# A hybrid decoder step on one core: the router's weights loaded through GpSimd's queue, and the last expert block's down product in four input slices

## The reference, cut to what matters

```python
mk, mv = _mem_kv(mem_prompt, norm_mem_g, w_ck, w_cv, ck_norm_g)       # memory keys and values
z = _rms(x, norm_g) @ w_in                                            # 2048 x 3584
...
lg = (h @ w_rg) + b_rg            # w_rg: 2048 x 4,  router over 4 groups
le = (h @ w_re) + b_re            # w_re: 2048 x 32, router over 32 experts
...
def expert_block(args):           # 2048 -> 512 -> 2048
    xe, e = args
    a = jax.nn.silu(xe @ w_e_gate[e]); b = xe @ w_e_up[e]
    return (a * b) @ w_e_down[e]
y = zeros.at[buf_t].add(yb * buf_g[:, None])
```

## Time and profile before

| | us |
|---|---|
| median of 3 runs | 1541.58 |
| lowest, highest run | 1539.56, 1543.03 |
| the profiled execution's own time | 1531.4 |
| its span in the trace | 1529.6 |
| PE busy | 1269.7 (83%) |
| DVE busy | 531.1 (35%) |
| ACT busy | 167.7 (11%) |
| POOL busy | 62.6 (4%) |

### The profile page before, as it was taken

The page is one execution under the profiler, slowest core; times in us unless marked ns, Lnnn a source line. Parts: engine busy times, 40 slices in busy tenths (PEclk is TensorE's granted clock), DMA queues, the critical chain, the costliest instruction groups (busy, mean ns, idle before and its releaser), DMA issues.

```text
span 1529.6 us, 23145 instructions
## 1 busy us (share of the span) xinstructions
PE 1269.7 (83%) x9913; PEld 626.5 (41%) x9913; DVE 531.1 (35%) x1102; ACT 167.7 (11%) x395; POOL 62.6 (4%) x115
## 2 busy tenths in 40 slices
PE   7799999998999999887867777777787677778777
PEld 4354458774887866322222222222222222222222
DVE  1040064750112334534334333433433433333344
ACT  0410012321111244000000000000000000000000
POOL 2000012212010000000000000000000000000000
PEclk9899999999999999988888788878887878778789
DMA  9999999989999999999999999999999999999997
GB/s 346 316 332 399 327 329 382 382 311 375 379 399 400 359 389 355 403 429 426 429 433 426 430 432 431 425 429 434 425 429 434 425 429 434 425 429 429 431 428 309
DMA packets 101909, 609.34 MB, mean 398 GB/s; under 512 B 11390, under 2 KB 13065, under 8 KB 78929
## 3 DMA queue, kind: packets, MB, share of 16 engines
q1 hardware_dynamic: 55027, 477.14, 75.0%
q10 hardware_dynamic: 38822, 101.11, 18.1%
q0 software_dynamic: 8016, 30.46, 5.7%
HBM read 603.09 MB, written 106.75 MB: 464 GB/s over the span
## 4 chain that ended last, share of the span: by engine, by line
DMA 53%; PE 40%; ACTq 3%; DVE 1%; issue 1%; ACT 1%; SPq 1%; DVEq 0%
DMA ring<-in_w_e_up_dram 44%; PE pb L1157 12%; PE pb L663 6%; PE pb L909 6%; DMA ring<-in_w_out_dram 5%; DMA ring<-in_w_in_dram 4%; PE pb L745 4%; ACTq L1286 2%; PE pb L1041 2%; PE pb L927 2%; PE pb L713 1%; SPq L486 1%; PE pb L669 1%; PE pb L1016 1%; PE pb L1191 1%
## 5 line engine op out<-in xcount | busy, mean ns | idle before, releaser
L1157 PE MATMUL pb<-ring,xT 128*32 128x256 f32 x4096 | 285.7, 441 | 123.4 <-DMA ring<-in_w_e_up_dram 118.7
L1157 PEld LDWEIGHTS pb<-ring,xT 128*32 128x32 f32 x4096 | 143.5, 126 | 285.7 <-DMA ring<-in_w_e_up_dram 156.5
L2040 DVE TENSOR_TENSOR Z<-pb,Z 128x512 f32<-128x512 f32 x248 | 152.7, 679 | 253.1 <-PE pb L1110 253.1
L1093 PE MATMUL pb<-Z,xT 128*32 128x512 f32 (+1 forms) x768 | 137.1, 808 | 94.8 <-DVE Z L2040 91.7
L1110 PE MATMUL pb<-xT 32*128 32x512 f32 x744 | 168.7, 751 | 0.0
L1191 PE MATMUL pb<-ring,xT 128*32 128x512 f32 x960 | 136.9, 722 | 0.0
L663 PE MATMUL pb<-ring,hreg 128*128 128x512 f32 (+1 forms) x320 | 125.7, 552 | 2.6 <-DMA ring<-in_w_in_dram 2.6
L1093 PEld LDWEIGHTS pb<-Z,xT 128*32 128x32 f32 (+1 forms) x768 | 16.6, 117 | 185.7 <-DVE Z L2040 118.9
L663 PEld LDWEIGHTS pb<-ring,hreg 128*128 128x128 f32 x320 | 60.1, 190 | 65.1 <-issue 59.2
L909 PE MATMUL pb<-hreg,ring 128*128 128x264 f32 x320 | 78.3, 402 | 5.8 <-DMA ring<-in_w_out_dram 5.8
L745 PE MATMUL pb<-hreg,ring 128*128 128x264 f32 x320 | 75.3, 395 | 1.0 <-DMA ring<-in_w_in_dram 1.0
(11 more groups left out here) (333 smaller groups left out, 1117.2 us busy)
## 6 DMA issues: line engine op xcount, KB each, us to landing
ring<-in_w_e_gate_dram SPq DMA_DIRECT2D x61, 2048.0 KB, 18.6
ring<-in_w_e_up_dram SPq DMA_DIRECT2D x61, 2048.0 KB, 23.1
ring<-in_w_e_down_dram SPq DMA_DIRECT2D x30, 4096.0 KB, 18.9
out_win_k_sample_dram<-in_cache_win_k_dram ACTq DMA_DIRECT2D x24, 1536.0 KB, 15.4
out_win_v_sample_dram<-in_cache_win_v_dram ACTq DMA_DIRECT2D x24, 1536.0 KB, 14.0
ring<-in_w_in_dram SPq DMA_DIRECT2D x7, 4096.0 KB, 32.9
ring<-in_w_out_dram SPq DMA_DIRECT2D x4, 4096.0 KB, 32.7
out_win_k_sample_dram<-in_cache_win_k_dram ACTq DMA_DIRECT2D x8, 1488.0 KB, 15.0
```

Of the source, the lines that this page charges most:

```text
L1093: last = mm(pb[0][32 * c:32 * c + 32, :], pick[0:n, t, :], xn[0:n, t, 512 * c:512 * c + 512], start=(t == 0), stop=(t == 2))
L1157: last = mm(pb[1][32 * c:32 * c + 32, 0:256], XT[:, k, :], w[:, :, k8, P * c:P * c + P], start=(k == 0), stop=(k == KT - 1))
L2040: last = V.tensor_tensor(d, banks[c][:, :], d, ALU.add)
```

## The change

Three things change. The loads of w_rg, w_re and b_re go from ACT's queue to POOL's, behind the bias loads. The last block's down weights are loaded in four input slices over all 2048 columns, and PE multiplies all four column groups for a slice, then ACT copies the whole output at once and `results()` goes through the tiles one after the other; DVE's adds and SP's stores follow that order (both halves of tile 0, then tile 1). And PE multiplies the identity with itself 14 times ahead of the last block's gate and up products.

```diff
 SP
-            for q in range(4):
-                c, f = slice(1024 * (q // 2), 1024 * (q // 2) + 1024), slice(2 * (q % 2), 2 * (q % 2) + 2)
-                sp.dma_start(slot2.rearrange("p (k n) -> p k n", k=4)[:, f, c], w[:, f, c]).then_inc(last_landed[q], 16)
+            for f in range(4):
+                sp.dma_start(slot2[:, D * f:D * f + D], w[:, f]).then_inc(last_landed[f], 16)
...
-            for n, t, hf in ((1, 0, 0), (2, 1, 0), (3, 0, 1), (5, 1, 1)):
+            for n, t, hf in ((1, 0, 0), (2, 0, 1), (3, 1, 0), (5, 1, 1)):
 POOL
+            for w, lo, n in (("w_rg", 0, NG), ("w_re", NG, NE)):
+                pool.dma_start(wr[:, :, lo:lo + n], a[w][0].rearrange("(k p) n -> p k n", p=P)).then_inc(router_landed, 16)
+            pool.dma_start(b36[:, NG:36], a["b_re"].to_broadcast([P, NE])).then_inc(router_landed, 16)
             pool.wait_ge(pads_ready, 1)
 PE
-            def results(hf):
+            def results():
-                for t in ((0, 1), (0, 2, 1))[hf]:
+                for t in range(3):
                     if t == 2:
                         pe.wait_ge(x_final, 1)
-                    for c in range(4) if t == 2 else (2 * hf, 2 * hf + 1):
+                    for c in range(4):
                         ...
-                    last.then_inc(out_filled, 1)
+                        if c == 3 or c == 1 and t < 2:
+                            last.then_inc(out_filled, 1)
...
+                if last_of_all:
+                    for _ in range(14):
+                        mm(pb[1][:, 0:P], ident[:], ident[:], start=True, stop=True)
...
-                pe.wait_ge(last_landed[0], LAST_LANDED[0])
-                last_down(0, (0, 1), pb[3])
-                pe.wait_ge(last_landed[1], LAST_LANDED[1])
-                last_down(0, (2, 3), pb[3]).then_inc(dn_used, 1)
+                for f in range(4):
+                    pe.wait_ge(last_landed[f], LAST_LANDED[f])
+                    for c in range(4):
+                        last = mm(pb[3][32 * c:32 * c + 32, :], aT[:, 32 * f:32 * f + 32],
+                                  slot2[:, D * f + 512 * c:D * f + 512 * c + 512], start=(f == 0), stop=(f == 3))
+                last.then_inc(dn_used, 1)
                 pe.wait_ge(gt_ready, NE)
-                pe.wait_ge(last_landed[2], LAST_LANDED[2])
-                last_down(1, (0, 1), pb[2])
                 pe.wait_ge(y_added, 3 * (NE - 1))
                 pe.wait_ge(yo_ready, NE)
-                results(0)
-                pe.wait_ge(last_landed[3], LAST_LANDED[3])
-                last_down(1, (2, 3), pb[2]).then_inc(dn_used, 1)
-                pe.wait_ge(yo_ready, NE + 1)
-                results(1)
+                results()
 ACT
-            for w, lo, n in (("w_rg", 0, NG), ("w_re", NG, NE)):
-                act.dma_start(wr[:, :, lo:lo + n], a[w][0].rearrange("(k p) n -> p k n", p=P)).then_inc(router_landed, 16)
-            act.dma_start(b36[:, NG:36], a["b_re"].to_broadcast([P, NE])).then_inc(router_landed, 16)
             act.wait_ge(zeros_ready, 2)
...
-                act.wait_ge(dn_used, NE)
-                nc.scalar.copy(yo[0:64, :], pb[3][0:64, :]).then_inc(yo_ready, 1)
-                act.wait_ge(dn_used, NE + 1)
-                nc.scalar.copy(yo[64:P, :], pb[2][64:P, :]).then_inc(yo_ready, 1)
+                block_out(NE - 1)
 DVE
-                for n, (hf, t) in enumerate(((0, 0), (0, 1), (1, 0), (1, 2), (1, 1))):
-                    dve.wait_ge(out_filled, n + 1)
+                for n, hf, t in ((1, 0, 0), (2, 1, 0), (3, 0, 1), (5, 0, 2), (4, 1, 1)):
+                    dve.wait_ge(out_filled, n)
```

## The result

The changed kernel takes 1523.25 us (median of 4 runs, 1516.14 to 1531.43), the kernel before 1541.47 beside it (1539.56 to 1543.03): a ratio of 0.9893, 95% interval 0.9861 to 0.9926. That is 18.2 us less, where 9.7 were forecast. The profiled execution took 1516.14 us, 15.3 less than that of before.

What follows compares the result with a forecast made beforehand. Bound: TensorE work for 610 us, then expert weight loads; the change touches only the ends, the start held by ScalarE's 30.33 us issue. Start -10.7 plus end +1.0 gives -9.7: 1541.58 to 1531.9 us, range 1527.5 to 1538.5.

Steps and rivals of the forecast that it cites:

- What bounds the start: First 40 us: ScalarE's 30.33 us issue of L1286 delays squares and diagonals, leaving TensorE idle 9.86 us before L705.
- 3.64 us at half speed held 1.82 us of work at full speed, a gain of 1.82 us: Start, 53.02 to 56.7: without TensorE's stop the slow-clock stretch goes too, saving 1.82 us besides the idle 9.86.
- its deduction: Start: 1 us taken off the 11.7 us gain for short rows on the DMA engines, leaving -10.7 us.
- I take 1: Start: router loads' short rows beside cache copies and perhaps the second w_in piece cost 1 us, bounds 0 and 5.
- I take nothing: Start: earlier cache copies might delay the memory values' weights, losing up to 5 us; 0 was taken.
- The end: Last block: identity products cost 3.2 us, down product to last add gains 2.2; sum +1.0 us, bounds -0.7 and +2.5.
- I carry this over: Whole kernel: the runs' median stays 10.2 us above the profiled execution, giving 1531.9 us instead of 1521.7.
- 1.5 us for the spread of the runs: Whole kernel: allowance of 1.5 us for run spread in the range 1527.5 to 1538.5, given 0.82.
- the best of every bound: Forecast case's lower limit, -12.4 us, with both the start's and the end's bounds at their best.
- the shift was to travel through it: Between start and end: events release the work, so a shift of the start reaches the end if loads keep up.

Runs made afterwards that it cites:

- The front alone: Kernel before with only the three router loads moved from ScalarE's queue to POOL's: 1522.17 us, ratio 0.9913; a second time 1524.83 us, ratio 0.9912.
- the end alone: Changed kernel with the three router loads put back on ScalarE's queue, so only the last block differs from the kernel before: 1538.78 us, ratio 1.0021.
- the kernel with identity products in the wait: Kernel before with 42 identity products added between TensorE's bias products and its wait for the diagonals: 1533.99 us, ratio 0.9970.
- the first pair: First profiles of the changed kernel and the kernel before; the changed kernel's median was 1523.25 us against 1541.47, ratio 0.9893.
- the three comparisons: The same changed kernel measured three times beside the kernel before: 1523.25 us (ratio 0.9893), 1525.39 us (0.9933) and 1521.55 us (0.9905).

## Why the prediction was wrong in size and right in mechanism

*What bounds the start: right.* With the long issue gone, the squares, the diagonals and the scales follow as forecast; the idle 9.86 us are gone, with 9 us of cover at the diagonals instead of 1.5 to 5.4. The front alone carries the gain, the end alone loses, and with the lists on SP's queue ScalarE is free and the scales start at 43.34 all the same: what held the start up was ScalarE's issue.

*The step that failed: "3.64 us at half speed held 1.82 us of work at full speed, a gain of 1.82 us".* The mechanism is right (the kernel with identity products in the wait shows it by itself), the size was that of one execution. In four traces with the blocked start the slow stretch cost 1.7 to 5.0 us, 3.1 in the mean, and the wait before it ended 0.6 to 0.9 us later in the three others. The first w_in product comes at 93.2 to 97.2 with the start blocked (mean of four 95.3) and at 81.3 to 82.8 with it free (mean of eight 81.9): the start is worth 13.3 us, where the forecast had 11.7 before its deduction. Of the difference 1.3 us are the slow stretch, most of the rest the later end of the wait. Of the terms of the sum this one was off most, and still it makes only 1.6 of the 8.5 us by which the forecast fell short.

*"I take 1" for the short rows: too much.* TensorE's wait for the second w_in piece did not grow (0.81 us before, 0.18 after). A price of 3 to 6 us may be there at the first piece, where it is hidden. Its source was misread in part: with the short rows gone from the first 40 us, the window from 15 to 20 still moves only 291 GB/s in the changed kernel (269 before); that from 35 to 40 moves 378 (248 before).

*"The values' weights: I take nothing": right, but the wrong load was watched.* They land at 38.7 instead of 39.4. The copies, issued 19 us earlier, hit the next load instead, the first w_in piece (13.2 to 37.8 us), which the forecast took as a proof that copies do little. That piece was down to its last 3 us when the first copies came. It cost nothing by luck of 2 us of cover.

*The end: right.* Forecast +1.0; 26.88 against 26.15 in the first pair is +0.73, and over the six traces with the changed end (26.81 to 27.06) against the three of before and the first with the front alone (26.14 to 26.15) it is +0.8; the second with the front alone has 25.77. (The kernel that keeps the clock up is left out: there TensorE's restart waits for weights.) The identity instructions took 4.82 us (forecast 4.9), the first half behind them 3.66, the down product 3.64, each as forecast.

*"I carry this over": the 10.2 us between the profiled execution and the median.* That execution, 1531.4 us, was quicker than each of the 55 timed ones of before (the lowest 1531.52; medians from 1536.48 to 1541.47). The two later profiles of before took 1539.66 and 1536.83. A part of the 6 us by which it was quick is its short slow stretch: the failed step again. The difference to the kernel before, which is what was missed, does not hang on it.

*"1.5 us for the spread of the runs": too little.* The four runs of the changed kernel spread over 15.3 us, the interval of the ratio alone reaches from 11.4 to 21.4 us, and the three comparisons lie 7.1 us apart. The range's lower edge, 1527.5, was the best of every bound with this 1.5 us; in it the start could not turn out better than read from the first trace, and it did.

*What stays open.* The three comparisons gave -18.2, -11.1 and -16.7, in the mean -15.3. The terms as measured give -13.3 + 0.8 = -12.5. Between start and end lies a long stretch for which the forecast had no term of its own: the shift was to travel through it. The traces have, in us (mean and range):

| from, to | start blocked, 4 traces | start free, 8 traces |
|---|---|---|
| first w_in product, cross-attention product near 512 to 534 | 437.0 (435.5 to 438.9) | 434.3 (430.7 to 437.7) |
| that product, TensorE's restart | 972.5 (971.3 to 974.8) | 973.9 (971.3 to 976.7) |

So 2.7 us are won in the first part and 1.3 lost again in the second; at the restart the free traces are 14.7 us ahead. In both parts the ranges overlap, and an earlier start need not be the reason: two kernels that are in neither mean, with the clock kept up (first w_in product at 92.74) and with the lists on SP's queue (89.15), took 433.9 and 433.2 us for the first part, like the free ones.

Of the 8.5 us that the forecast missed, 2.8 are its own terms (start 1.6, short rows 1.0, end 0.2), 1.4 this stretch, 1.4 what the mean of the comparisons has beyond the traces, and 2.9 what the first comparison has beyond that mean. For the last three no cause is shown.

## What to carry to other kernels

Lists of some thousand short rows are paid by the engine that hands them out, here 30 us and more on two hardware queues and 2.9 on POOL's: look for one long issue bar, ask who needs that engine in the meantime, and move the list to the engine that nobody waits for; moved to another busy queue it only changes the victim. Before a term is taken from one trace, ask whether it depends on when something happened to start: a clock's slow stretch and waits for loads do, and want two or three traces. When a queue is unblocked, list everything that it will now send earlier, and look for the load that used to run alone.

## What the runs showed of the hardware

The same three loads made far more packets on the hardware queue than on POOL's. The DMA queues over the whole run (packets, MB, share), first before, then after:

```profile
q10 hardware_dynamic: 38822, 101.11, 18.1%
q0 software_dynamic: 8016, 30.46, 5.7%
```

```profile
q10 hardware_dynamic: 34550, 100.80, 17.9%
q0 software_dynamic: 8176, 30.78, 5.9%
```

4272 packets left ScalarE's queue and 160 came to POOL's, for the same 0.3 MB. On SP's queue (q1) the lists made 4272 packets too: 58787 in that run, 54515 in the changed kernel. With them went the long issue (30.33 us on ScalarE, 36.95 on SP, 1.16 on POOL) and the late landing (35.4, 47.8 and 14.6 us). The Trainium skill, page "DMA: Bandwidth & Descriptors", section "Issuing engine by pattern", calls the hardware path (SP and ScalarE) generally the faster one; for this list of short rows the trace disagrees, by more than twice.

One list alone does not show the long issue. In the kernel before, ScalarE handed out w_rg, of as many rows, in 0.41 us, and the long issue is that of the list behind it (timeline):

```profile
5.13 0.41 ACTq L1286 DMA_DIRECT2D wr<-in_w_rg_dram  x1
5.57 30.33 ACTq L1286 DMA_DIRECT2D wr<-in_w_re_dram  x1
35.94 3.18 ACTq L1287 DMA_DIRECT2D b<-in_b_re_dram  x1
```

SP's three issues have the same pattern: 0.47, 36.95 and 8.20 us. Whether w_re pays for its own rows or waits until those of w_rg are out of the way, no run here tells; nor was either list issued later, or alone, from ScalarE or SP.
